# First phase of a two-block network on one core: column sums on VectorE, another order of modulation and h, the first two products row by row of h, the step sizes' chain in five steps

## The chip, the cores and the metric
The kernel runs on one core of one Trainium2 chip. The metric is the time of one execution on the device, in microseconds; smaller is better. Three runs of the kernel before gave 2241.81, 2244.04 and 2248.78 us.

## What is computed
Two blocks one after the other on 512 tokens of 1024 features, in float32. The first block's beginning is what the change touches:
```python
mod = silu(c) @ w_mod + b_mod              # six vectors of 1024 (shift, scale, gate, twice)
mod_c = silu(c_ctx) @ w_mod + b_mod        # the same for the context
h_lat = rmsnorm(x, norm1_g) * (1 + sc1) + sh1         # 512 tokens
h_ctx = rmsnorm(ctx, norm1_g) * (1 + csc1) + csh1     # 256 tokens
p = h @ w_in                               # z | xbc | dt | q | k | v | gates
xbc = silu(dwconv3(p[xbc]))                # 3072 channels, of them xs 2048, B 512, C 512, in four groups
dt = softplus(p[dt] + dt_bias)             # 64 step sizes a token
la = dt * -exp(a_log)                      # log decays, summed in chunks of 128 tokens
```
Then follow, for each of four groups, a bidirectional scan over chunks (ten states, four output chunks), window attention, the merge, a convolutional FFN, and a second block with three branches. All of that is the same in both kernels.

## The kernel before
Features lie on the partitions, tokens on the free axis; LT is 512 latent plus 256 context tokens. Each weight is split in two float32r parts, whi (a cast by ScalarE, line 1171) and wlo (a subtraction by GpSimd, line 2389), and so is h (hT_h by ScalarE, line 1190; hT_l by VectorE, line 1634, or GpSimd, line 2406, by turns). A product is three matmuls for each 128x128 of weights: whi·hi, whi·lo, wlo·hi (lines 760 to 762; 776 to 778 for the narrow dt). One xbc block is 8 rows of h x 2 column ranges (512 and 256) x 3, 48 matmuls. Weights come in blocks of 128x1024 (512 KB) into raww, a ring of RAWS = 4 slots; a slot is free when GpSimd has made wlo, or, for the modulation (not split, line 893), when TensorE has read it. whi and wlo have PAIRS = 3 slots. SyncE issues the loads (line 2562).

order() writes one list of steps, and every engine goes through this list in order and does its part of each step; semaphores carry the rest. So what stands behind a step in the list waits for it on each engine that has a part in it. merge() mixes two lists of steps by costs given in SHARE. plan.upto[t] says up to which block the split parts are to be made before step t, and SyncE loads RAWS blocks further, at steps that own a block.

The list of the first phase: init; norm1 (eight squares on ScalarE, line 1185, each with six column sums on TensorE, line 790, two instructions each); rms (VectorE reduces and takes the inverse root, lines 1640 to 1660, with a power on GpSimd, line 2398; TensorE spreads it over the partitions, line 799); then for each modulation j of 0 to 3 four blocks mod(j, n), modt (ScalarE copies the row, line 1228), xnorm (after j = 0; eight multiplications on VectorE, line 1845), modsel (TensorE turns the row, line 901) and modout (VectorE, lines 1851, 1857; for j = 2 and 3 it makes A1, the scale of h). 0 and 1 are shifts, 2 and 3 scales; 0 and 2 serve rows 0 to 3 of h, 1 and 3 rows 4 to 7. Then h1(0) to h1(7): hv = A1·x + shift on VectorE (lines 1869, 1870; rows 1, 4, 7 on ScalarE, lines 1236, 1237), its cast and its low part. Then four steps dt merged with the six xbc products of group 0:
```text
dt0  xbc0  xbc1  taps0 conv0  dt1  xbc2  taps1 conv1  xbc3  dt2
taps2 conv2  xbc4  taps3 conv3  dt3  xbc5  taps4 conv4  taps5 conv5
```
dt0 is the narrow product, dt1 (line 911) turns it and holds the whole softplus chain of VectorE and ScalarE (lines 1878 to 1886, 1694 to 1707), dt2 the cumulated sums (lines 916 to 918, 1890 to 1896), dt3 turns these (line 923), copies them (line 1899) and has ScalarE store them with eight DMAs (lines 1261, 1265). taps (lines 1199, 1686, 1689) and conv (1288, 1917) are the depthwise convolution and silu; taps reads the product's PSUM banks and frees them. The products take banks in turn out of four (0, 1, 2, 7), two for each xbc block (one for xbc5), so a product waits for the taps of the one two places before.
Behind it stand the transpositions xt, bt, the ten states of group 0 (line 947; VectorE lines 1734, 1937, 1942) with xbc(1,0) and xbc(1,1) among them, then the four chunks with cap (1958), decay (1313), cbm, cscale (1964), scale (1970), out (967 to 970), keep (1978) and xbc(1,2) to xbc(1,5) among them.

## Time and profile before
| | |
|---|---|
| runs | 2241.81, 2244.04 (median), 2248.78 us |
| profiled execution | 2248.61 us, its span 2247.3 us, mean granted clock 0.959 |
| busy | TensorE 2067.4, VectorE 1058.7, ScalarE 860.4, GpSimd 819.7 us |
| chain that ended last | TensorE 79%, VectorE 11%, ScalarE 4%, DMA 2% |
| DMA | 235.65 MB, mean 105 GB/s |

The span runs from the first to the last instruction of the program; the execution's own time is 1.3 us longer. A row of a timeline gives the start, the time from the first start to the last end of equal instructions in a row, the engine, the line, and in brackets how long the engine had been idle and what ended that. "PEclk" is the clock granted to TensorE, as a share of 2.4 GHz: 0.50 is 1.2 GHz. In a row of stages each engine has its busy time and its count of instructions.

### The profile page before, as it was taken

The page shows a single profiled execution, that of the slowest core. Times are in us where ns is not written, and L with a number is a line of the kernel's source. Part 1 is how long each engine was busy: PE and PEld are TensorE (multiplying, and loading weights), DVE is VectorE, ACT ScalarE, POOL GpSimd, SP SyncE. Part 2 cuts the span into 40 slices and gives each one's busy share as a digit, 9 for nine tenths or more (in the row PEclk, how much of TensorE's full clock was granted, in tenths as well). Part 3 has the DMA queues.
Part 4 walks back from the last instruction along what each step waited for, and adds up shares of the span by engine and source line. Part 5 has one row for each costly group of instructions (what it writes and reads, how often), then busy time and mean ns, then how long its engine had stood idle before and what let it go on. Part 6 is the DMA issues. An engine that isn't in the chain of part 4 may idle for free.

```text
span 2247.3 us, 28706 instructions
## 1 busy us (share of the span) xinstructions
PE 2067.4 (92%) x11668; PEld 1673.7 (74%) x11668; DVE 1058.7 (47%) x1735; ACT 860.4 (38%) x1561; POOL 819.7 (36%) x455
## 2 busy tenths in 40 slices
PE   6777999998999999999899999988889988989997
PEld 5565778786877787888787888876667766768886
DVE  1437776858555554542344442137544664521112
ACT  1333444444444444323343443233544443422221
POOL 0321121211353322456444444443531451554442
PEclk8788999999999999999999999989999999989998
DMA  6231544545321112523334333334121222333331
GB/s 218 82 124 52 185 160 159 162 152 184 127 71 38 38 48 83 180 94 103 94 114 143 101 100 94 96 120 127 47 68 53 83 60 84 97 97 96 94 101 63
DMA packets 89252, 235.65 MB, mean 105 GB/s; under 512 B 27424, under 2 KB 30624, under 8 KB 88224
## 3 DMA queue, kind: packets, MB, share of 16 engines
q1 hardware_dynamic: 85712, 225.16, 31.3%
q10 hardware_dynamic: 3408, 8.65, 1.0%
q8 instruction: 92, 1.51, 0.3%
q14 instruction: 40, 0.33, 0.0%
HBM read 220.51 MB, written 12.19 MB: 104 GB/s over the span
## 4 chain that ended last, share of the span: by engine, by line
PE 79%; DVE 11%; ACT 4%; DMA 2%; issue 1%; POOL 1%; ACTq 0%; SPq 0%; DVEq 0%; POOLq 0%
PE ps L760 20%; PE ps L761 20%; PE ps L762 20%; PE ps L1053 1%; PE ps L1112 1%; PE ps L947 1%; PE ps L1040 1%; PE ps L1028 1%; PE ps L893 1%; PE ps L790 1%; PE ps L969 1%; PE ps L967 1%; PE ps L968 1%; PE ps L1131 1%; PE ps L970 1%
## 5 line engine op out<-in xcount | busy, mean ns | idle before, releaser
L2389 POOL TENSOR_TENSOR wlo<-raww,whi 128x1024 fp32r<-128x1024 f32 (+2 forms) x254 | 593.8, 2344 | 1003.7 <-ACT whi L1171 999.3
L1171 ACT CAST whi<-raww 128x1024 fp32r<-128x1024 f32 (+2 forms) x284 | 285.0, 1006 | 262.9 <-PE ps L762 190.0
L760 PE MATMUL ps<-hT_h,whi 128*128 128x512 f32 (+1 forms) x704 | 268.7, 382 | 22.3 <-DVE xsc__81 L1689 19.0
L762 PE MATMUL ps<-hT_h,wlo 128*128 128x512 f32 (+1 forms) x704 | 259.6, 369 | 0.0
L761 PE MATMUL ps<-hT_l,whi 128*128 128x512 f32 (+1 forms) x704 | 259.5, 369 | 0.0
L760 PE MATMUL ps<-H_h,whi 128*128 128x512 f32 x480 | 192.3, 401 | 18.0 <-POOL wlo L2389 9.6
L761 PE MATMUL ps<-H_l,whi 128*128 128x512 f32 x480 | 188.6, 393 | 0.0
L762 PE MATMUL ps<-H_h,wlo 128*128 128x512 f32 x480 | 188.1, 392 | 0.0
L760 PEld LDWEIGHTS ps<-hT_h,whi 128*128 128x128 f32 x704 | 135.7, 193 | 49.7 <-DVE xsc__81 L1689 20.0
L761 PEld LDWEIGHTS ps<-hT_l,whi 128*128 128x128 f32 x704 | 135.4, 192 | 23.6 <-issue 2.9
L762 PEld LDWEIGHTS ps<-hT_h,wlo 128*128 128x128 f32 x704 | 135.0, 192 | 22.2
L1727 DVE SCALAR_TENSOR_TENSOR gt<-gt,ps 128x512 f32<-128x512 f32 x40 | 27.5, 687 | 254.3 <-PE ps L762 254.3
L760 PE MATMUL ps<-h_h,whi 128*128 128x512 f32 x336 | 132.1, 393 | 0.8 <-ACT mk L1450 0.8
L761 PE MATMUL ps<-h_l,whi 128*128 128x512 f32 x336 | 131.0, 390 | 0.0
L762 PE MATMUL ps<-h_h,wlo 128*128 128x512 f32 x336 | 130.8, 389 | 0.0
L760 PEld LDWEIGHTS ps<-H_h,whi 128*128 128x128 f32 x480 | 91.5, 191 | 42.1 <-issue 12.1
L762 PEld LDWEIGHTS ps<-H_h,wlo 128*128 128x128 f32 x480 | 91.1, 190 | 19.6
L761 PEld LDWEIGHTS ps<-H_l,whi 128*128 128x128 f32 x480 | 91.3, 190 | 18.7 <-issue 0.5
L1313 ACT ACTIVATE ec<-ec,la 128x128 f32<-128x128 f32 x256 | 76.9, 388 | 58.5 <-DVE ec L1958 58.5
L1686 DVE SCALAR_TENSOR_TENSOR ua<-ps,vc,ua 128x511 f32<-128x511 f32 x44 | 33.0, 750 | 110.1 <-ACT ua L1199 110.1
L1712 DVE TENSOR_REDUCE small<-ps 128x1 f32<-128x513 f32 (+1 forms) x64 | 48.3, 755 | 72.5 <-PE ps L1033 52.9
L760 PEld LDWEIGHTS ps<-h_h,whi 128*128 128x128 f32 x336 | 63.1, 188 | 15.8 <-issue 1.6
(500 smaller groups left out, 4678.7 us busy)
## 6 DMA issues: line engine op xcount, KB each, us to landing
ec<-csd SPq DMA_DIRECT2D x32, 1024.0 KB, 8.0
raww<-in_w_mod SPq DMA_DIRECT2D x48, 512.0 KB, 4.9
raww<-in_w_up SPq DMA_DIRECT2D x44, 512.0 KB, 3.7
raww<-in_w_xbc SPq DMA_DIRECT2D x24, 512.0 KB, 4.5
raww<-in_w_gl SPq DMA_DIRECT2D x24, 512.0 KB, 3.5
raww<-in_w_z SPq DMA_DIRECT2D x16, 512.0 KB, 4.4
raww<-in_w_g SPq DMA_DIRECT2D x16, 512.0 KB, 3.5
raww<-in_w_os SPq DMA_DIRECT2D x16, 512.0 KB, 3.6
```

Source lines behind the costliest of these rows:

```text
L760: e.matmul(o, whi[:, i, c], hi(k)[:, t0:t1], start=(k == 0), stop=False)
L761: e.matmul(o, whi[:, i, c], lo(k)[:, t0:t1], start=False, stop=False)
L762: last = e.matmul(o, wlo[:, i, c], hi(k)[:, t0:t1], start=False, stop=(k == kt - 1))
L790: last = e.matmul(ps[:, b, o:o + 1], x[:, t * 128:(t + 1) * 128], ones[:, 0:1], start=True, stop=True)
L893: last = e.matmul(ps[32 * q:32 * q + 32, b, 0:128], cs_[:, 4 * n + 2 * kk:4 * n + 2 * kk + 32], raww[:, p % RAWS, kk * 512 + q * 128:kk * ...
L947: e.matmul(ps[:, b, :], Btok[:, CHUNKS[d][n], :], xw[:, i, :], start=True, stop=True).then_inc(*ssd_done.mark(("state", g, d, n), ("free", ...
L1171: e.copy(whi[:, i, 0:n], raww[:, p % RAWS, 0:n]).then_inc(*w_high.mark(("high", p)))
L1313: last = e.activation(E[:, r, :], E[:, r, :], ACT.Exp, bias=la[:, c, h:h + 1])
L1686: e.scalar_tensor_tensor(out=dst[:, 1:T], in0=psum[:, 0:T - 1], scalar=V(names[0], m), in1=dst[:, 1:T], op0=ALU.mult, op1=ALU.add).then_in ...
L1712: e.tensor_reduce(sm[:, 1:2], S, AXX, ALU.max, negate=True).then_inc(*v_step.mark(event))
L1727: e.scalar_tensor_tensor(out=x, in0=x, scalar=1.0, in1=psum, op0=ALU.add, op1=ALU.mult).then_inc(*v_moved.mark(*events))
L2389: e.tensor_tensor(wlo[:, i, 0:n], raww[:, p % RAWS, 0:n], whi[:, i, 0:n].bitcast(F32), ALU.subtract).then_inc(*p_wlow.mark(("split", p), ( ...
```

## The change
1. Squares: the seven additions of the eight squares go to VectorE (acc1), and TensorE forms six column sums of the total in a step total of its own. The reduction on VectorE goes.
2. Order: modulation 0, then 2, 1, 3, with norm, root, xnorm (now one step a row), h rows and their split in between. The modulations 0 to 3 take banks 3 and 4.
3. bring: the blocks of w_dt and of xbc(0,0) are loaded before the last four modulation blocks and split there. Before dtx 2 no other block is split.
4. dtx 0 to 3 replace the narrow product and xbc(0,0): each takes two rows of h for both. w_dt's low part is written beside its high part into whi, so one matmul with hi gives whi·hi in rows 0 to 63 and wlo·hi in rows 64 to 127, and dt1 adds the halves as it turns them (12 matmuls for 6 transposes).
5. The chain of the step sizes is cut: 0 copies, 1 turn, abs, exp, 2 one plus, ln, 3 reciprocal up to ln step, 4 the cumulated sums, 5 their turn and store.
6. SHARE has other costs for groups 0 and 1, and one xbc step of group 1 instead of two among the states.

The list becomes (numbers as in the code; m is mod):
```text
init norm1 m(0,0) m(0,1) m(0,2) total m(0,3) modt0 m(2,0) m(2,1) modsel0 modout0 rms m(2,2) m(2,3) modt2
xnorm0 xnorm1 m(1,0) modsel2 modout2 m(1,1) h0 xnorm2 m(1,2) h1 xnorm3 m(1,3) modt1 h2 xnorm4 bring h3 xnorm5
m(3,0) modsel1 modout1 m(3,1) xnorm6 dtx0 m(3,2) xnorm7 m(3,3) modt3 dtx1 modsel3 modout3 h4 h5 dtx2 h6 h7 dtx3
dt0 xbc1 taps0 conv0 dt1 xbc2 taps1 conv1 dt2 xbc3 taps2 conv2 dt3 xbc4 taps3 conv3 dt4 xbc5 dt5 taps4 conv4 taps5 conv5
xt4 xt5 xbc(1,0) bt xt0..3, ten states, cb cap decay cap decay xbc(1,1) cbm cscale scale out(0,0) taps(1,0) conv(1,0)
xbc(1,2) ... keep0 out(0,1) ... xbc(1,3) ... out(0,2) xbc(1,4) ... xbc(1,5) keep2 out(0,3) ... xt(1,4) and on as before
```
```diff
+         "state": 9.6, "cap": 0.54, "cbm": 0.9, "scale": 3.8, "out": 4.8, "keep": 1.45, "xbc": 4.0, "taps": 0.05,
+         "conv": 2.5, "z": 1.65, "zgate": 0.77, "zsum": 0.7, "mod": 2.25, "score": 1.66, "pt": 1.12, "pv": 0.82,
...
 def ssd_states(g):
-    t = [(SHARE["xt"], [("xt", g, 4), ("xt", g, 5)]), (SHARE["bt"], [("bt", g)]), (SHARE["xt"], [("xt", g, c) for c in range(4)])]
...
 def xbc_steps(g):
...
-    o = [("init",), ("norm1",), ("rms", "in")]
-    for j in range(4):
-        o += [("mod", j, n) for n in range(4)] + [("modt", j)] + ([("modsel", j - 1), ("modout", j - 1)] if j else [("xnorm",)])
-    o += [("modsel", 3), ("modout", 3)]
-    o += [("h1", k) for k in range(8)]
-    o += merge([(8.0, [("dt", i)]) for i in range(4)], xbc_steps(0))
+    mod = lambda j: [[("mod", j, n)] for n in range(4)]
+    a, b, c, d = mod(0), mod(2), mod(1), mod(3)
+    o = [("init",), ("norm1",)] + a[0] + a[1] + a[2] + [("total", "in")] + a[3] + [("modt", 0)]
+    o += b[0] + b[1] + [("modsel", 0), ("modout", 0), ("rms", "in")] + b[2] + b[3] + [("modt", 2), ("xnorm", 0), ("xnorm", 1)]
+    o += c[0] + [("modsel", 2), ("modout", 2)] + c[1] + [("h1", 0), ("xnorm", 2)] + c[2] + [("h1", 1), ("xnorm", 3)]
+    o += c[3] + [("modt", 1), ("h1", 2), ("xnorm", 4), ("bring",), ("h1", 3), ("xnorm", 5)]
+    o += d[0] + [("modsel", 1), ("modout", 1)] + d[1] + [("xnorm", 6), ("dtx", 0)] + d[2] + [("xnorm", 7)] + d[3] + [("modt", 3), ("dtx", 1)]
+    o += [("modsel", 3), ("modout", 3), ("h1", 4), ("h1", 5), ("dtx", 2), ("h1", 6), ("h1", 7), ("dtx", 3)]
+    o += merge([(SHARE["dt"], [("dt", i)]) for i in range(6)], xbc_steps(0))
     x = xbc_steps(1)
-    o += [("load", 0), ("load", 1)] + merge(ssd_states(0), x[:2]) + merge(ssd_chunks(0), x[2:])
...
-    if s == ("dt", 0):
-        return [(("w_dt", 0, 0, 512), 512, True)]
+    if s == ("bring",):
+        return [(("w_dt", 0, 0, 512), 512, True), (("w_xbc", 0, 0, 1024), 1024, True)]
...
+        for t, s in enumerate(self.order):
             mine = blocks_of(s)
             if mine:
...
+                if t < start:
+                    n = base if s[0] == "bring" else n
+                else:
+                    n = max(n, min(self.split_at[more - 1] + 1 if more <= len(self.split_at) else len(self.blocks), base + RAWS - 1))
+                load = max(load, n + RAWS, base + RAWS)
             elif s[0] == "duo" and s[3] == 7:
                 n = max(n, min(self.split_at[done + AHEAD - 1] + 1, base + RAWS - 1))
...
+                n = self.split_at[done + AHEAD - 2] + 1
+                load = n + RAWS
             self.upto.append(n)
+            self.loads.append(load)
         spans = {s: t for t, s in enumerate(self.order)}
         a, b = spans["s5tab", 0], spans["fence", "glu"]
...
+        sq1, acc1 = sbuf("sq1", [P, 4, LT], 136), sbuf("acc1", [P, LT], 148)
...
-                elif k == "norm1":
-                    for j in range(8):
-                        add_up("in", j, ["in"])
+                elif k == "total" and s[1] == "in":
+                    b = bank(("stat", s[1]), (5,))
+                    PE.wait_ge(at("squares", s[1]))
+                    for t in range(6):
+                        last = e.matmul(ps[:, b, t:t + 1], acc1[:, t * 128:(t + 1) * 128], ones[:, 0:1], start=True, stop=True)
...
+                elif k == "dtx":
+                    x = ("xbc", 0, 0)
+                    pd, px = plan.first["dt", 0], plan.first[x]
+                    if s[1] == 0:
+                        banks = [bank((u, t0), ring_of_gemms[0]) for u in (("dt", 0), x) for t0, _ in ALL]
+                        PE.wait_ge(at("split", pd))
+                        PE.wait_ge(at("split", px))
+                    else:
+                        banks = [bank_of((u, t0)) for u in (("dt", 0), x) for t0, _ in ALL]
+                    wd, wx = plan.pair[pd] % PAIRS, plan.pair[px] % PAIRS
+                    hi, lo = PAIR["hT"]
+                    two = (2 * s[1], 2 * s[1] + 1)
+                    end = s[1] == 3
+                    for q in two:
+                        PE.wait_ge(at("pair", "hT", q))
+                        c = slice(q * 128, (q + 1) * 128)
+                        for (t0, t1), b in zip(ALL, banks[2:]):
+                            o = ps[:, b, 0:t1 - t0]
+                            e.matmul(o, whi[:, wx, c], hi(q)[:, t0:t1], start=(q == 0), stop=False)
+                            e.matmul(o, whi[:, wx, c], lo(q)[:, t0:t1], start=False, stop=False)
+                            last = e.matmul(o, wlo[:, wx, c], hi(q)[:, t0:t1], start=False, stop=(q == 7))
+                            if q == 7:
+                                last.then_inc(*gemm_done.mark(("gemm", x, t0), *[("used", px)] * (t1 == LT)))
+                    for (t0, t1), b in zip(ALL, banks[:2]):
+                        for q in two:
+                            if q:
+                                e.matmul(ps[0:64, b, 0:t1 - t0], whi[:, wd, q * 128:q * 128 + 64], lo(q)[:, t0:t1], start=False, stop=False)
+                            last = e.matmul(ps[:, b, 0:t1 - t0], whi[:, wd, q * 128:q * 128 + 128], hi(q)[:, t0:t1], start=(q == 0), stop=(q == 7))
+                            if q == 0:
+                                e.matmul(ps[0:64, b, 0:t1 - t0], whi[:, wd, 0:64], lo(0)[:, t0:t1], start=False, stop=False)
+                        if end:
+                            last.then_inc(*gemm_done.mark(("gemm", ("dt", 0), t0), *[("used", pd)] * (t1 == LT)))
+                elif k == "xbc" and s[1:] == (0, 0):
+                    pass
                 elif k == "dt":
-                    if s[1] == 0:
-                        narrow(s, 64, "hT", ALL)
-                    elif s[1] == 1:
+                    if s[1] == 1:
                         b = bank("dtok", (4,))
                         PE.wait_ge(at("dt rows"))
                         for c in range(6):
-                            last = e.transpose(ps[:, b, c * 64:c * 64 + 64], dtT[:, c * 128:c * 128 + 128], ident[0:64, 0:64])
+                            e.matmul(ps[:, b, c * 64:c * 64 + 64], dtT[:, c * 128:c * 128 + 128], ident[:, 0:64], start=True, stop=False)
+                            last = e.matmul(ps[:, b, c * 64:c * 64 + 64], dtT[:, c * 128:c * 128 + 128], ident[:, 64:128], start=False, stop=True)
                         last.then_inc(*turned.mark(("dt turned",)))
...
+                    o = halves(i)[:, :, 0:64] if p == plan.first["dt", 0] else whi[:, i, 0:n]
+                    x = raww[:, p % RAWS, 0:n]
+                    e.copy(o, x.rearrange("p (k c) -> p k c", c=64) if p == plan.first["dt", 0] else x).then_inc(*w_high.mark(("high", p)))
...
+                        ACTE.wait_ge(at("modulation turned", {2: 0, 1: 2, 3: 1}.get(j, j - 1)))
...
-                            e.copy(dtT[:, t0:t1], ps[0:64, bank_of((s, t0)), 0:t1 - t0]).then_inc(
+                            e.copy(dtT[:, t0:t1], ps[:, bank_of((s, t0)), 0:t1 - t0]).then_inc(
...
+                        ACTE.wait_ge(at("abs", "dt"))
+                        e.activation(flat(csm), flat(csm), ACT.Exp, scale=-1.0).then_inc(*a_func.mark(("exp abs", "dt")))
+                    elif s[1] == 2:
+                        ACTE.wait_ge(at("one plus", "dt"))
+                        e.activation(flat(etot), flat(wdec), ACT.Ln).then_inc(*a_func.mark(("ln", "dt")))
+                    elif s[1] == 3:
                         ACTE.wait_ge(at("step kept off zero"))
                         e.activation(lndt[:, :, :], lndt[:, :, :], ACT.Ln).then_inc(*a_func.mark(("ln step",)))
-                    elif s[1] == 2:
...
+                elif k == "norm1":
+                    for j in range(1, 8):
+                        DVE.wait_ge(at("square", "in", j - 1) + at("square", "in", j))
+                        after_last()
+                        e.tensor_tensor(acc1[:, :], acc1[:, :] if j > 1 else sq1[:, slot("sq1", ("in", 0)), :],
+                                        sq1[:, slot("sq1", ("in", j)), :], ALU.add).then_inc(
+                            *v_made.mark(("free", "sq1", ("in", j)), *[("free", "sq1", ("in", 0))] * (j == 1), *[("squares", "in")] * (j == 7)))
                 elif k == "xnorm":
+                    j = s[1]
...
-                    for j in range(8):
-                        e.tensor_tensor(xin[:, j, :], xin[:, j, :], r, ALU.mult).then_inc(
-                            *v_moved.mark(("x normed", j), *[("out of", ("rms", "in"))] * (j == 7)))
+                    e.tensor_tensor(xin[:, j, :], xin[:, j, :], r, ALU.mult).then_inc(
+                        *v_moved.mark(("x normed", j), *[("out of", ("rms", "in"))] * (j == 7)))
...
-                        softplus("dt", flat(dt_), flat(csm), flat(wdec), flat(etot))
+                        after_last()
+                        e.scalar_tensor_tensor(out=u, in0=x, scalar=-1.0, in1=x, op0=ALU.mult, op1=ALU.max).then_inc(*v_step.mark(("abs", "dt")))
+                    elif s[1] == 2:
+                        DVE.wait_ge(at("exp abs", "dt"))
+                        e.tensor_scalar(w, u, 1.0, None, ALU.add).then_inc(*v_step.mark(("one plus", "dt")))
+                        after_last()
+                        e.scalar_tensor_tensor(out=u, in0=w, scalar=-1.0, in1=u, op0=ALU.add, op1=ALU.subtract).then_inc(*v_step.mark())
+                    elif s[1] == 3:
+                        DVE.wait_ge(at("ln", "dt"))
+                        after_last()
+                        e.reciprocal(w, w).then_inc(*v_step.mark())
+                        after_last()
+                        e.scalar_tensor_tensor(out=u, in0=u, scalar=-1.0, in1=w, op0=ALU.mult, op1=ALU.mult).then_inc(*v_step.mark())
...
-                    e.tensor_tensor(wlo[:, i, 0:n], raww[:, p % RAWS, 0:n], whi[:, i, 0:n].bitcast(F32), ALU.subtract).then_inc(
-                        *p_wlow.mark(("split", p), ("raw free", p)))
+                    o, x, h = wlo[:, i, 0:n], raww[:, p % RAWS, 0:n], whi[:, i, 0:n]
+                    if p == plan.first["dt", 0]:
+                        o, x, h = halves(i)[:, :, 64:128], x.rearrange("p (k c) -> p k c", c=64), halves(i)[:, :, 0:64]
...
-                if plan.upto[t] and s in plan.first:
-                    load_weights(plan.upto[t] + RAWS)
+                if s in plan.first or s == ("dtx", 2):
+                    load_weights(plan.loads[t])
```

## Rows read from the trace of the kernel before
**Rows 1.** The page: engines' busy; the splits' groups (busy, mean ns of one).
```profile
PE 2067.4 (92%) x11668; PEld 1673.7 (74%) x11668; DVE 1058.7 (47%) x1735; ACT 860.4 (38%) x1561; POOL 819.7 (36%) x455
...
L2389 POOL TENSOR_TENSOR wlo<-raww,whi 128x1024 fp32r<-128x1024 f32 (+2 forms) x254 | 593.8, 2344 | 1003.7 <-ACT whi L1171 999.3
...
L1171 ACT CAST whi<-raww 128x1024 fp32r<-128x1024 f32 (+2 forms) x284 | 285.0, 1006 | 262.9 <-PE ps L762 190.0
```
**Rows 2.** Stages: length, PE, PEld, DVE, ACT, POOL busy, PEclk, DMA share, GB/s.
```profile
18.20:35.40 17.20, 14.54 (x67) 14.26 (x67) 0.88 (x5) 0.84 (x1) 1.33 (x1) 1.00 0.00 1
...
40.40:63.10 22.70, 14.71 (x200) 8.90 (x192) 4.87 (x9) 2.36 (x5) 3.50 (x2) 0.50 0.93 328
...
63.10:81.30 18.20, 10.48 (x23) 4.31 (x24) 9.76 (x15) 11.07 (x15) 7.90 (x6) 0.50 0.13 45
...
77.90:81.30 3.40, 3.32 (x8) 1.48 (x9) 0.79 (x1) 1.86 (x3) 2.38 (x2) 0.50 0.00 0
...
84.50:92.84 8.34, 8.34 (x50) 7.38 (x49) 0.00 (x0) 1.32 (x2) 2.39 (x1) 1.00 0.35 117
...
92.80:166.60 73.80, 59.32 (x313) 50.12 (x311) 30.27 (x52) 27.19 (x45) 14.26 (x6) 0.91 0.28 93
...
166.60:191.40 24.80, 18.88 (x68) 10.93 (x69) 17.00 (x25) 1.38 (x2) 2.34 (x1) 0.98 0.16 54
...
191.40:254.80 63.40, 53.82 (x434) 47.53 (x432) 57.24 (x78) 34.65 (x89) 10.61 (x4) 0.90 0.40 125
...
322.00:2247.00 1925.00, 1810.92 (x10009) 1470.37 (x10008) 887.74 (x1467) 746.71 (x1337) 760.52 (x424) 0.97 0.31 100
```
**Rows 3.** Timeline, 9 to 63 us: column sums, spread, xnorm, A of modout 3.
```profile
9.27 20.64 PE L790 MATMUL ps<-cst,sq 128*128 128x1 f32 x96 [9.27 <-DMA cst<-in_consts]
...
32.58 2.93 PE L799 MATMUL ps<-cst,nst 128*128 128x128 f32 x12 [2.66 <-DVE nst L1646]
...
35.55 7.00 DVE L1845 TENSOR_TENSOR xin<-xin,ps 128x768 f32<-128x768 f32 x8 [3.02 <-PE ps L799]
...
61.83 1.39 DVE L1857 SCALAR_TENSOR_TENSOR A<-modS,vc 128x8 f32<-128x8 f32 x1
```
**Rows 4.** Timeline of the h rows: low parts, the last narrow matmul's wait.
```profile
64.90 0.96 DVE L1634 TENSOR_TENSOR hT_l<-hv,hT_h 128x768 fp32r<-128x768 f32 x1 [0.90 <-ACT hT_h L1190]
...
67.02 1.81 POOL L2406 TENSOR_TENSOR hT_l<-hv,hT_h 128x768 fp32r<-128x768 f32 x1 [3.82 <-ACT hT_h L1190]
...
67.71 1.93 DVE L1634 TENSOR_TENSOR hT_l<-hv,hT_h 128x768 fp32r<-128x768 f32 x1 [1.07 <-ACT hT_h L1190]
...
80.80 0.68 PE L776 MATMUL ps<-hT_h,whi 128*64 128x512 f32 x1
```
**Rows 5.** Timeline of PE: products of group 0 behind waits, dt3's transposes.
```profile
115.24 0.56 PE L760 MATMUL ps<-hT_h,whi 128*128 128x512 f32 x1 [4.84 <-DVE xsc__81 L1689]
...
132.18 0.77 PE L760 MATMUL ps<-hT_h,whi 128*128 128x512 f32 x1 [5.45 <-DVE xsc__81 L1689]
...
142.36 0.60 PE L923 MATMUL ps<-cst,csm 128*64 128x128 f32 x4
...
152.62 0.50 PE L760 MATMUL ps<-hT_h,whi 128*128 128x512 f32 x1 [3.30 <-DVE BTs L1689]
```
**Rows 6.** Timeline of ACT: a table load, the issues of dt3's eight stores.
```profile
103.62 1.28 ACT L1196 ACT_TABLE_LOAD   x1
...
143.72 2.66 ACTq L1261 DMA_DIRECT2D csd<-csT  x4
...
147.08 2.10 ACTq L1265 DMA_DIRECT2D csd<-ecsT  x4
```
**Rows 7.** Timeline of DVE in the states: the wait behind xbc(1,1).
```profile
184.64 0.69 DVE L1942 TENSOR_TENSOR st<-stt__90,ps 128x512 f32<-128x512 f32 x1 [5.91 <-PE ps L947]
```
**Rows 8.** Chunks: a stage as in rows 2, and PE's wait for taps(1,0).
```profile
199.50:250.20 50.70, 47.37 (x360) 41.57 (x360) 49.36 (x67) 27.45 (x69) 10.61 (x4) 0.92 0.47 147
...
202.03 0.77 PE L760 MATMUL ps<-hT_h,whi 128*128 128x512 f32 x1 [8.69 <-DVE xsc__81 L1689]
```

69 lines of the change are left out of this document (41 added, 28 removed), and 4 rows, old and new, of the table SHARE.

## The prediction
> **What bounds the kernel now.** I read the engines' totals first: TensorE is busy for 92% of the span, no other engine for half of it [rows 1]. The table of stages comes second. After 322 us TensorE works 1811 us of 1925, at 0.97 of its clock, and nothing of the change lies there; those 1925 us are carried over as they are. What an edit of the first phase can reach lies before about 255 us, and there the table shows different stages [rows 2]. (a) 18.2 to 35.4 us: the DMA share is 0.00. All four slots of raww hold modulation blocks that TensorE has not read, since it forms column sums until 29.9 and then waits for the root. (b) 40.4 to 63.1: DMA at 0.93, TensorE at half clock: the modulation is paced by its weights. (c) 63.1 to 81.3: the eight rows of h are made, TensorE busy 10.5 of 18.2. (d) 92.8 to 166.6: five products of group 0 and the step sizes' chain, TensorE busy 59 of 74. (e) 166.6 to 191.4: ten states, a chain on VectorE. (f) 191.4 to 254.8: four chunks, VectorE busy 57 of 63. The waits in the timelines come third; they give the single terms.
>
> **Part 1: from the start to the end of the first xbc product, 92.8 us now.** Removed: the 48 column sums (96 instructions) that fill 9.3 to 29.9 [rows 3]. Added: seven additions of 128x768 on VectorE. A subtraction of that shape with both operands in SBUF takes 0.96 [rows 4], so 6.7 us; some of them fit before the second half of x has landed, and I let the last end at 18.2, when the four modulation blocks are there too, for DMA goes quiet at 18.2 [rows 2]. Six sums remain, 12 instructions at 20.64/96 = 0.215, so 2.6 us: 20.8.
> Modulation 0 and half of 2 are multiplied as they land. The root stands behind modout 0 on VectorE, at about 23.5, and costs 2.5 (29.9 to 32.6 now, less the reduction that goes); the spread takes 2.9 at full clock, up to 5.9 at half [rows 3]; I take 4.2: 30.2. On TensorE mod(2,2) and mod(2,3) are queued behind this spread, and with them the slots, so DMA pauses again for some 3 us.
> Then VectorE works in order: two rows of xnorm (7.00/8 = 0.88 each), modout 2 with its A (1.4) [rows 3], at about 33.8. Rows of h take 17.7/8 = 2.2 each now (63.1 to 80.8 [rows 4]), and an xnorm mostly fits into VectorE's waits for ScalarE's casts: rows 0 to 2 by 40.4. On ScalarE the casts of w_dt and of the first xbc block stand behind row 2, on GpSimd their low parts follow, for 1024 columns 1.0 and 2.34, for 512 about half of each [rows 1]: 1.5 and 2.3 after row 2, dtx 0 may start at 44.3.
> One dtx covers two rows. For xbc it is six 128x512 and six 128x256 matmuls; for dt the wlo product now sits in the idle 64 columns of a pass, so it is four of each instead of six. At half clock eight 128x512 take 3.4 us, 0.43 each [rows 2], a 256 half of it: 10 x 0.64 = 6.4 us for one dtx, and 3.2 at full clock. The clock was back at 81.3, after 3.3 us of work [rows 2]. So a dtx behind idle time costs about 4.9, one behind work 3.2. dtx 0 ends at 49.2. The last two modulation blocks reuse the slots of w_dt and xbc, freed at 42 to 44, and land at 47 to 49: 50.5. modsel 3 is queued behind dtx 1: 53.9. modout 3 and its A: 55.7. Rows 4 to 7: four times 2.2, and 1.0 for the cast of block 18 and 1.1 for its low part, which are queued before row 6's cast and row 7's low part: 10.9. dtx 2 runs from 62.4 to 67.3, dtx 3 to 70.5. I take **71**, against 92.8: **21.8 gained**. Bounds: 14 more blocks (7.1 MB) after 18.2 at stage (b)'s 328 GB/s [rows 2] end at 40, and with the tail (1 + 2 + 10.9 + 3.2) the product ends at 57; with all four dtx at half clock it ends at 80.
>
> **Part 2: from there to the first state product, 73.8 us now.** The step sizes' chain stood in one step between xbc products, and the taps that free TensorE's banks were queued behind it. TensorE waits 4.84, 5.45 and 3.30, and after each wait the product takes 10.2 (132.18 to 142.36 [rows 5]) where an undisturbed one takes 8.34 [rows 2]: 13.6 + 5.6 = 19.2 us. With five steps the longest piece is the one from the reciprocal to the clamp, some 5.5 us, and the taps come in time within 8.34. Exp, Tanh and Ln alternate more often, two more table loads of 1.28 on ScalarE [rows 6], which is busy 27 of 74 us [rows 2]: hidden; 2.6 without this cover.
> Two waits are new or larger. (1) xbc(0,1) takes the banks of dt, which ScalarE copies only after dtx 3: 1.1 us (hidden by xbc(0,0) now). (2) The last step (transposes, csT, eight stores that ScalarE issues) now stands behind xbc(0,5) instead of before it. ScalarE needs 5.5 us for it (143.72 to 149.18 [rows 6]), and taps(0,4), whose bank xbc(1,0) takes, are queued behind. From the transposes' end (142.96) to xbc(1,0) at 152.62 are 9.7 us [rows 5], and 6.4 of them are TensorE's work now: xbc(0,5) and a transposition. After the change only the transposition, 1.0, lies in it: a wait of 8.7, and a cold product behind (+1.9). Twelve instead of six narrow products turn dt: +0.5. Sum: -19.2 + 1.1 + 8.7 + 1.9 + 0.5 = **7.0 gained**. Bounds: 18 gained if wait (2) doesn't come, 2 lost if old waits stay.
>
> **Part 3: the ten states, 24.8 us now.** xbc(1,1) moves out of them. VectorE waits 5.91 for a state queued behind this product on TensorE [rows 7]; else it needs 2.0 a state. **5.9 gained.** TensorE then idles between all states, but the stage shows 0.98 of the clock with it [rows 2]; I cost that at nothing. Bounds 2 and 7.5.
>
> **Part 4: the four chunks, 63.4 us now.** xbc(1,1) comes here, between the caps and the first output, into the 8.69 that TensorE waits there for taps(1,0) behind ScalarE's decays [rows 8]. TensorE's work: 53.8 busy now [rows 2], less 1.9 for the product that was cold behind that wait, plus 8.4, is 60.3. VectorE's is 57.2, and between 199.5 and 250.2 it is busy 49.4 of 50.7 [rows 8]. Two full engines, each in order: I add 1.2, 61.5, **1.9 gained**. Bounds: 60.3 and 68.
> The steps behind are the same, and nothing there goes by absolute time.
> The Trainium skill has a rule that speaks against more work on VectorE ("SBUF — State Buffer", section "SBUF: two separate sides"): a VectorE operation with two SBUF inputs and a GpSimd operation that reads SBUF exclude each other for the whole instruction. The trace agrees: the same low part takes 0.96 alone and 1.93 when GpSimd has begun one before it [rows 4]. For the seven additions it changes nothing, since GpSimd is idle then; by it each new meeting in parts 1 and 4 would cost about 1 us, which the bounds hold.
>
> **Sum.** 21.8 + 7.0 + 5.9 + 1.9 = 36.6 us. The profiled execution has a span of 2247.3 us and took 2248.6; it would be 2210.7 and 2212.0. It lies 4.6 above the median of the runs, so against 2244.0 the forecast is **2207.5 us**.
>
> **The rivals.** *A, the weights' stream decides the first phase.* The slots never run out and part 1 ends near 60, or wait (2) isn't there: 11 us more in either case, **2196.5**. For it: the stream could end at 40. Against: root and spread stand before mod(2,2) on TensorE, and two slots wait for GpSimd. *B, a cold first phase.* The clock stayed at 0.50 from 63.1 to 81.3 with TensorE busy 10.5 of 18.2 us [rows 2]. If products row by row keep it there, every dtx costs 6.4, +9.4, and a few us of VectorE's meetings with GpSimd come in part 4: **2221**. The Trainium skill ("TensorE: Matmul & The Clock Gate", section "Part 1: The HAM clock gate") says that half rate is the default and that activity lifts it; by it, the removal of the column sums leaves TensorE at half clock from the start, where stage (a) shows full clock, and B is what follows. *C, the modulation isn't ahead.* The slots stay taken, by the spread in the queue and by the wait for GpSimd's low parts, mod(3,3) still ends near 57, and wait (2) eats the rest: 5 us gained, **2239**. *D, slower.* One mechanism: the clock does not come back behind dtx 3, and products of 8.4 us in parts 2 and 4 run at half. Each costs 8.4 more; from the fifth on (42 against 36.6) the kernel is slower than before, seven give **2266**. Against it: from 84.5 dense products held 1.00, and (d) to (f) 0.90 and more [rows 2].
>
> **How the numbers follow.** Forecast 0.47 (2200 to 2216), A 0.23 (below 2200), B 0.20, C 0.06, D 0.04. The range takes in B and most of A with their bounds, **2190 to 2227**, and leaves out C, D and the lowest part of A. A measurement of this kernel can tell about 0.3% (7 us) from no change: faster 0.92, same 0.05, slower 0.03.
>
> **What would show it.** Part 1: w_mod's first 16 issues end near 44, the A of modout 3 ends near 55.7, the first xbc product near 71. Part 2: no wait of TensorE over 2 us between xbc(0,1) and xbc(0,5), then one of 8 to 9 before xbc(1,0), behind ScalarE's eight stores. Part 3: ten states in 19 us, without a wait of 5.9. Part 4: no wait of 8.7, 60 to 63 us. The prediction is wrong if the work behind xt(1,4) takes another time than now, or if a dense stretch shows a granted clock of 0.50.

## The result and the profile after

The changed kernel took 2208.76 us (median of four runs, 2205.08 to 2210.52), the kernel before, measured beside it, 2244.35; the ratio is 0.9837, 95% interval 0.9817 to 0.9857. The forecast was 2207.5, range 2190 to 2227.

The profiled execution of after is the fastest of its runs, 2205.1 us with a span of 2203.7, while that of before (2248.6) was 4.3 above its median. So the two traces differ by 43.5 us, the medians by 35.6. The page of after, busy times and the group of GpSimd's splits (compare [rows 1]: no engine's work has changed by more than 2% of itself):
```profile
PE 2035.2 (92%) x11586; PEld 1651.1 (75%) x11586; DVE 1060.8 (48%) x1741; ACT 862.6 (39%) x1563; POOL 821.7 (37%) x455
...
L2483 POOL TENSOR_TENSOR wlo<-raww,whi 128x1024 fp32r<-128x1024 f32 (+2 forms) x253 | 594.3, 2355 | 945.3 <-ACT whi L1237 941.0
```
The stages of after (columns as in [rows 2]): the first two reach to the root's spread, the next two to the copies of dt, then one each for the prediction's parts 2, 3 and 4, and the rest.
```profile
0.00:15.50 15.50, 0.00 (x0) 0.00 (x1) 5.35 (x20) 6.15 (x9) 0.30 (x5) 1.00 0.93 327
15.50:30.50 15.00, 12.06 (x126) 9.86 (x130) 3.93 (x9) 1.70 (x3) 1.33 (x1) 1.00 0.79 276
30.50:58.40 27.90, 16.85 (x207) 13.05 (x206) 15.29 (x21) 6.80 (x11) 7.63 (x4) 0.76 0.63 217
58.40:73.40 15.00, 9.99 (x40) 7.92 (x40) 3.52 (x6) 7.59 (x12) 6.66 (x3) 0.77 0.12 37
73.40:140.10 66.70, 58.13 (x329) 50.23 (x329) 30.84 (x52) 30.61 (x48) 16.76 (x7) 0.95 0.34 111
140.10:156.90 16.80, 11.95 (x21) 3.48 (x22) 14.86 (x24) 0.41 (x1) 0.00 (x0) 0.90 0.13 44
156.90:218.40 61.50, 58.50 (x482) 52.12 (x480) 59.82 (x79) 35.72 (x90) 13.80 (x5) 1.00 0.42 138
...
218.40:2203.70 1985.30, 1867.73 (x10391) 1514.48 (x10390) 927.15 (x1533) 773.61 (x1392) 775.22 (x430) 0.97 0.32 102
```
The DMA share tells the main thing: where before had 17 us at 0.00 [rows 2], after has 0.93, 0.79 and 0.63 up to 58.4. The four parts against their forecasts, in us:

| part | before | after | forecast |
|---|---|---|---|
| 1, to the first product's end | 92.8 | 73.4 | 71 |
| 2, to the first state product | 73.8 | 66.7 | 66.8 |
| 3, ten states | 24.8 | 16.8 | 18.9 |
| 4, four chunks, to xt(1,4) | 63.4 | 61.5 | 61.5 |
| sum | 254.8 | 218.4 | 218.2 |
| behind it | 1992.5 | 1985.3 | 1992.5 |

Part 1 in the timeline of after (PE, DVE, POOL, ACT; columns as in [rows 3]):
```profile
15.53 2.27 PE L921 MATMUL ps<-raww,cs__56 128*32 128x128 f32 x32 [15.53 <-DMA raww<-in_w_mod]
...
19.01 2.72 PE L855 MATMUL ps<-cst,acc 128*128 128x1 f32 x12
...
27.58 2.93 PE L824 MATMUL ps<-cst,nst 128*128 128x128 f32 x12 [2.61 <-DVE nst L1716]
30.44 1.76 PE L921 MATMUL ps<-raww,cs__56 128*32 128x128 f32 x48
...
42.48 2.43 DVE L1943 TENSOR_SCALAR hv<-xin,A,modS 128x256 f32<-128x256 f32 x1
...
42.24 2.52 POOL L2483 TENSOR_TENSOR wlo<-raww,whi 128x1024 fp32r<-128x1024 f32 x1
...
47.64 0.79 PE L952 MATMUL ps<-hT_h,whi 128*128 128x512 f32 x1 [4.18 <-DVE xin L1918]
...
58.20 0.17 DVE L1930 SCALAR_TENSOR_TENSOR A<-modS,vc 128x8 f32<-128x8 f32 x1
...
72.50 0.86 ACT L1310 COPY dtT<-ps 128x512 f32<-128x512 f32 x2 [5.46 <-PE ps L961]
```
The modulation starts at 15.5 instead of 35.4 and the spread is through at 30.5. The first dtx then waits 4.18 us, and not for its weights: these are split at 42.24 + 2.52 = 44.76. It waits for VectorE's last xnorm (L1918), which reads bank 7. Part 2 has the wait that was forecast, before xbc(1,0), behind ScalarE's eight issues and the activations of taps(0,4) (PE, then ACT and its queue):
```profile
117.73 1.09 PE L994 MATMUL ps<-cst,xsc__82 128*128 128x128 f32 x8 [0.78 <-DVE csT L1990]
125.67 0.80 PE L785 MATMUL ps<-hT_h,whi 128*128 128x512 f32 x1 [6.85 <-DVE BTs L1755]
...
117.71 2.71 ACTq L1332 DMA_DIRECT2D csd<-csT  x4
...
121.12 2.10 ACTq L1336 DMA_DIRECT2D csd<-ecsT  x4
123.27 1.23 ACT L1265 ACTIVATE BTs<-ps,vc 128x512 f32<-128x512 f32 x2 [2.18 <-issue]
```
The waits of [rows 5] (4.84, 5.45, 3.30), of [rows 7] (5.91) and of [rows 8] (8.69) are gone.

### The profile page after: what moved, and what is told of

It is laid out like the page before. It is cut to its first block, busy times and chain, and to the rows that moved or that the text cites. A ratio compares the mean times of both kernels' runs of the same rounds, so it can differ in the third digit from the quotient of the medians.

```text
span 2203.7 us, 28555 instructions
## 1 busy us (share of the span) xinstructions
PE 2035.2 (92%) x11586; PEld 1651.1 (75%) x11586; DVE 1060.8 (48%) x1741; ACT 862.6 (39%) x1563; POOL 821.7 (37%) x455
## 4 chain that ended last, share of the span: by engine, by line
PE 79%; DVE 12%; ACT 4%; DMA 1%; issue 1%; POOL 1%; ACTq 0%; SPq 0%; DVEq 0%; POOLq 0%
PE ps L785 20%; PE ps L786 20%; PE ps L787 20%; PE ps L1117 1%; PE ps L1104 1%; PE ps L1176 1%; PE ps L1011 1%; PE ps L1092 1%; PE ps L921 1%; PE ps L1033 1%; DVE ec L2049 1%; PE ps L1031 1%; PE ps L1195 1%; PE ps L1032 1%; PE ps L1158 1%
## 5 line engine op out<-in xcount | busy, mean ns | idle before, releaser
L785 PE MATMUL ps<-hT_h,whi 128*128 128x512 f32 (+1 forms) x688 | 261.1, 379 | 7.4 <-DVE BTs L1755 6.8
L787 PE MATMUL ps<-hT_h,wlo 128*128 128x512 f32 (+1 forms) x688 | 252.4, 367 | 0.0
L786 PE MATMUL ps<-hT_l,whi 128*128 128x512 f32 (+1 forms) x688 | 252.3, 367 | 0.0
L1778 DVE TENSOR_REDUCE small<-ps 128x1 f32<-128x513 f32 (+1 forms) x64 | 48.3, 755 | 72.5 <-PE ps L1097 52.9
```

Of the source, the lines that this page charges most:

```text
L785: e.matmul(o, whi[:, i, c], hi(k)[:, t0:t1], start=(k == 0), stop=False)
L786: e.matmul(o, whi[:, i, c], lo(k)[:, t0:t1], start=False, stop=False)
L787: last = e.matmul(o, wlo[:, i, c], hi(k)[:, t0:t1], start=False, stop=(k == kt - 1))
L1778: e.tensor_reduce(sm[:, 1:2], S, AXX, ALU.max, negate=True).then_inc(*v_step.mark(event))
```

## Experiments

Each kernel below was profiled, so they can be compared by four places in their timelines as well as by the whole time: the start of dt's copies (ScalarE, L1310 in after), the first state product, the first product cb behind the states, and xt(1,4), behind which the step list is the same everywhere. The whole time is uncertain by some 4 us, the places by up to 1.9: after, e1, e7 and e8 have the same list up to dt's copies, which start at 72.5, 74.4, 74.0 and 74.2. What differs first between these four is when TensorE gets its full clock: at 31.0 us in after, at 32.8 to 33.3 in the other three. There the three modulation blocks behind the spread take 2.76 to 2.79 instead of the 1.76 above (TensorE's timeline of e1):
```profile
30.11 2.79 PE L923 MATMUL ps<-raww,cs__56 128*32 128x128 f32 x48
```
and GpSimd's low part of the first xbc block ends 0.7 to 0.9 later than in after. The clock also rose late in e3 and e11, and early in e2 and e10.

| run | median us | ratio to before (95%) | dt copies | state | cb | xt(1,4) | behind |
|---|---|---|---|---|---|---|---|
| before | 2244.35 | 1 | 82.0 | 166.6 | 191.4 | 254.8 | 1992.5 |
| after | 2208.76 | 0.9837 (0.9817–0.9857) | 72.5 | 140.1 | 156.9 | 218.4 | 1985.3 |
| e1_store_late | 2202.65 | 0.9799 (0.9779–0.9818) | 74.4 | 136.2 | 152.9 | 214.5 | 1988.2 |
| e2_turn_first | 2203.20 | 0.9803 (0.9777–0.9829) | 68.8 | 136.2 | 153.0 | 214.5 | 1988.8 |
| e3_bank7_free | 2206.98 | 0.9820 (0.9795–0.9845) | 70.9 | 138.5 | 156.0 | 216.8 | 1988.9 |
| e4_root_behind_mod2 | 2206.01 | 0.9816 (0.9791–0.9841) | 73.2 | 141.0 | 158.5 | 219.2 | 1985.9 |
| e5_sums_on_pe | 2224.06 | 0.9903 (0.9881–0.9925) | 87.8 | 155.5 | 173.0 | 233.8 | 1989.1 |
| e6_before_sums_dve | 2238.72 | 0.9960 (0.9946–0.9973) | 75.0 | 159.7 | 184.5 | 248.1 | 1989.2 |
| e7_chain_one_step | 2218.33 | 0.9876 (0.9849–0.9903) | 74.0 | 151.9 | 169.5 | 230.2 | 1985.8 |
| e8_old_states | 2217.97 | 0.9874 (0.9847–0.9901) | 74.2 | 142.0 | 166.4 | 229.5 | 1986.7 |
| e9_products_behind_h | 2203.27 | 0.9806 (0.9788–0.9824) | 66.7 | 134.1 | 150.9 | 212.4 | 1988.5 |
| e10_three_edits | 2196.36 | 0.9778 (0.9765–0.9791) | 65.8 | 127.5 | 144.3 | 205.8 | 1987.4 |
| e11_four_edits | 2196.52 | 0.9778 (0.9765–0.9791) | 67.3 | 129.1 | 146.6 | 207.4 | 1987.8 |
| e12_before_again | 2246.46 | – | 83.2 | 167.8 | 192.7 | 256.2 | 1988.9 |

In before and e6 the copies of dt come before the first xbc product (half of them, for the second follows at 84.7 in before), so this column compares only kernels with dtx.

**e1_store_late**: the wait in part 2.
```diff
+    o.remove(("dt", 5))
+    o.insert(o.index(("conv", 0, 4)) + 1, ("dt", 5))
```


> The changed kernel with one step moved: dt5 (turn and store of the sums) stands behind conv(0,4) in the list, so ScalarE makes taps(0,4) before it issues the eight stores. Theory (the wait of 6.85 us before xbc(1,0) is the store's issues in front of the taps): this wait falls under 1 us, the cold product behind it is gone (+1.9), the first state product starts at 131 to 133 us instead of 140.1, and 8 us reach xt(1,4) (210). Rival (the states need the stored sums anyway): the wait only moves to the first state, which starts at 138 to 140; xt(1,4) within 2 us of 218.4.


From the copies of dt to the first state product it takes 61.8 us instead of 67.6: 5.8 gained, where about 8 were expected (3.9 at xt(1,4), since this execution's copies of dt started 1.9 later). No wait before xbc(1,0) is left; what remains, and was not expected, in TensorE's timeline of e1, is the wait of the transposes for the copy of the turned sums:
```profile
121.36 1.36 PE L996 MATMUL ps<-cst,xsc__82 128*128 128x128 f32 x8 [2.54 <-DVE csT L1992]
```
The position of this one step in the list was the cause of the 6.85.

**e2_turn_first**: dtx 1 stood before modsel 3.
```diff
-    ... d[3] + [("modt", 3), ("dtx", 1)]
-    o += [("modsel", 3), ("modout", 3), ("h1", 4), ("h1", 5), ("dtx", 2), ...
+    ... d[3] + [("modt", 3)]
+    o += [("modsel", 3), ("modout", 3), ("dtx", 1), ("h1", 4), ("h1", 5), ("dtx", 2), ...
```


> The changed kernel with dtx 1 behind modsel 3 and modout 3 instead of before them. Theory (A of rows 4 to 7 is late because its turn is queued behind dtx 1 on TensorE): A ends near 55 instead of 58.4 and everything behind is 3.4 us earlier, xt(1,4) at 215. Rival (TensorE has no gap to put dtx 1 in): 0 to 1 us.


A of modout 3 comes 3.6 us earlier than the 58.20 of after, the copies of dt 3.7, xt(1,4) 3.9 (VectorE's timeline of e2):
```profile
54.61 0.17 DVE L1930 SCALAR_TENSOR_TENSOR A<-modS,vc 128x8 f32<-128x8 f32 x1
```
Two matmuls of 8 columns decide when rows 4 to 7 of h begin; a product of 3.6 us in front of them passes on in full.

**e3_bank7_free**: what the first dtx waits for.
```diff
-                        spread(("rms", n), 3, LT, (6,), at("root", n))
+                        spread(("rms", n), 3, LT, (5,), at("root", n))
```
The spread then lies in banks 5 and 6 instead of 6 and 7.


> The changed kernel with the spread of the root in banks 5 and 6 instead of 6 and 7. Theory (dtx 0 starts at 47.6 and not at 44.8, where its low part is ready, because its fourth bank, 7, is part of the spread that xnorm(7) reads last): dtx 0 starts at 44.8 and xt(1,4) comes 2 to 2.9 us earlier. Rival (the last two modulation blocks then set the pace, their slots are freed by GpSimd): dtx 0 earlier, the A of modout 3 unchanged at 58.4, xt(1,4) unchanged.


TensorE's timeline of e3, the first matmul of dtx 0:
```profile
45.55 0.77 PE L952 MATMUL ps<-hT_h,whi 128*128 128x512 f32 x1 [1.82 <-POOL wlo L2483]
```
dtx 0 now waits for GpSimd's low part, and no longer for the bank. The copies of dt come only 1.6 us earlier than in after, less than the 2 to 2.9 expected and inside the scatter of the places. But the clock rose late here, so the low part ended 0.7 later (45.45). Beside e1, e7 and e8, where the clock rose as late, dtx 0 starts 2.8 to 3.0 us earlier and the copies come 3.1 to 3.5 earlier. So the bank was the cause, and about 3 us is what it was worth. The whole times of e3 and after can't be told apart.

**e4_root_behind_mod2**: do the slots behind the spread cost anything?
```diff
-    o += b[0] + b[1] + [("modsel", 0), ("modout", 0), ("rms", "in")] + b[2] + b[3] + ...
+    o += b[0] + b[1] + [("modsel", 0), ("modout", 0)] + b[2] + b[3] + [("rms", "in")] + ...
```


> The changed kernel with the root and its spread behind mod(2,3) instead of before mod(2,2). Theory (the spread in TensorE's queue holds two raw slots and stops the DMA): the blocks of w_dt and xbc are issued 3 us earlier, the A of modout 3 ends 2 to 3 us earlier, xt(1,4) near 216. Rival (the path through part 1 is VectorE's xnorm and h rows, which wait for the spread): everything 1.5 to 2 us later, xt(1,4) near 220.


mod(3,3) ends at 54.54 (54.13 in after) and xt(1,4) is 0.8 later, which is inside the scatter: no gain, and no loss that could be told either. The spread comes no later than in after (27.74 against 27.58), and GpSimd's low part ends at 44.60 (44.76 in after), since ScalarE casts these weights behind row 2 of h in both. So the slots held by the spread cost nothing that shows. The run also tells something of the clock, since here TensorE's granted clock rose early. Two stages of e4:
```profile
18.50:21.80 3.30, 2.50 (x48) 2.22 (x44) 0.00 (x0) 0.27 (x1) 0.00 (x0) 1.00 0.91 339
21.80:32.00 10.20, 7.89 (x80) 5.90 (x80) 2.12 (x7) 0.27 (x1) 1.33 (x1) 0.50 0.85 280
```
and TensorE's timeline in them:
```profile
18.50 1.50 PE L855 MATMUL ps<-cst,acc 128*128 128x1 f32 x12
...
27.74 2.93 PE L824 MATMUL ps<-cst,nst 128*128 128x128 f32 x12
```
The spread takes 2.93 in a stretch that is recorded at 0.50, exactly as in after (27.58) and in before [rows 3], and the six sums take 1.50 in a stretch at 1.00 where they take 2.72 in after. I come back to this below.

**e5_sums_on_pe**: the changed kernel with the 48 column sums on TensorE.
```diff
-    o = [("init",), ("norm1",)] + a[0] + a[1] + a[2] + [("total", "in")] + a[3] + [("modt", 0)]
+    o = [("init",), ("norm1",)] + a[0] + a[1] + a[2] + a[3] + [("modt", 0)]
...
+                elif k == "norm1":
+                    for j in range(8):
+                        add_up("in", j, ["in"])
```
(and in VectorE's program the seven additions go, the reduction comes back)


> The changed kernel with the 48 column sums back on TensorE (no additions on VectorE, the reduction back), all else as changed. Theory (the sums hold TensorE until 29.9 us and with it the raw slots and the root): the first modulation product starts at 30 instead of 15.5, the root 5 us later, the last modulation block and the A of modout 3 about 8 us later, first state product near 148, and about 8 us are lost at xt(1,4). Rival (the later weights' stream or VectorE catches up): less than 3 us at xt(1,4).


The column sums and the spread in TensorE's timeline of e5:
```profile
9.13 20.64 PE L815 MATMUL ps<-cst,sq 128*128 128x1 f32 x96 [9.13 <-DMA cst<-in_consts]
...
41.75 2.93 PE L824 MATMUL ps<-cst,nst 128*128 128x128 f32 x12 [2.93 <-DVE nst L1713]
```
15.4 us later at xt(1,4), twice what I expected. I had priced the sums as in the old order, where the root stands before the modulation. In the new one it stands behind six of its blocks, so with the sums at 29.7 all of it starts 14.2 later (29.70 against 15.53) and the spread 14.2 later (41.75 against 27.58).

**e6_before_sums_dve**: the same edit alone, in the kernel before.
```diff
-                    for j in range(8):
-                        add_up("in", j, ["in"])
+                    for t in range(6):
+                        last = e.matmul(ps[:, b, t:t + 1], acc1[:, t * 128:(t + 1) * 128], ones[:, 0:1], start=True, stop=True)
```
(and the seven additions on VectorE)


> The kernel before with this one part of the change: squares added on VectorE, six column sums on TensorE. Theory: all of the first phase starts 8.2 us earlier (29.9 to 21.7), first state product at 158.4 instead of 166.6, xt(1,4) at 246.6 instead of 254.8. Rival (without the sums TensorE is at half clock and the modulation slower): under 4 us.


The six sums, the spread and the first modulation in TensorE's timeline of e6:
```profile
19.02 2.69 PE L830 MATMUL ps<-cst,acc 128*128 128x1 f32 x12 [19.02 <-DVE acc L1843]
24.05 2.93 PE L799 MATMUL ps<-cst,nst 128*128 128x128 f32 x12 [2.33 <-DVE nst L1649]
26.91 3.48 PE L896 MATMUL ps<-raww,cs__56 128*32 128x128 f32 x64
```
Alone it gains 6.7 us at xt(1,4) (8.2 expected; 2238.7, ratio 0.996), less than half of the 15.4 that it is worth in the new order. Additions on VectorE and modulation ahead of the root are worth more together.

**e7_chain_one_step**: the step sizes' chain in one step and where it stood.
```diff
+    for i in (2, 3, 4, 5):
+        o.remove(("dt", i))
+    i = o.index(("dt", 1)) + 1
+    o[i:i] = [("dt", 2), ("dt", 3)]
+    o.insert(o.index(("xbc", 0, 3)) + 1, ("dt", 4))
+    o.insert(o.index(("xbc", 0, 5)), ("dt", 5))
```


> The changed kernel with the step sizes' chain in one piece behind dt1 and the sums' steps where the kernel before has them. Theory (the forecast's part 2): waits of 4.8, 5.4 and 3.3 us come back, that of 6.85 goes, 7 us are lost, first state product at 147. Rival (the new wait eats what the cut gains): within 2 us of 140.1.


Waits of products in TensorE's timeline of e7:
```profile
99.56 0.77 PE L791 MATMUL ps<-hT_h,whi 128*128 128x512 f32 x1 [5.02 <-DVE xsc__82 L1761]
...
117.19 0.77 PE L791 MATMUL ps<-hT_h,whi 128*128 128x512 f32 x1 [5.45 <-DVE xsc__82 L1761]
137.90 0.50 PE L791 MATMUL ps<-hT_h,whi 128*128 128x512 f32 x1 [3.31 <-DVE BTs L1761]
```
The three waits of [rows 5] are back to within 0.2 us, the one of 6.85 is gone, and from the copies to the first state product it takes 77.9 instead of 67.6: 10.3 lost, against 7 expected (the first state product comes at 151.9, not 147).

**e8_old_states**: two products of group 1 before and among the states again.
```diff
-SHARE = {"dt": 2.4, "x1": 1.2, "state0": 10.56, "xbc0": 5.76, "xbc1": 13.1, "taps0": 0.05, "taps1": 0.01,
-         "conv0": 4.0, "conv1": 2.4, "xt0": 2.6, "bt0": 0.91, "cap0": 0.54, "out0": 11.93, "xt": 2.6, "bt": 0.55,
+SHARE = {"dt": 2.4, "x1": 2, "xbc0": 5.76, "taps0": 0.05,
+         "conv0": 4.0, "xt": 2.6, "bt": 0.55,
```


> The changed kernel with the old list from the states of group 0 on (xbc(1,1) among the states). Theory: the states take 24.8 us instead of 16.8 and the chunks 63.4 instead of 61.6, so xt(1,4) at 228. Rival (the chunks, with VectorE at 95%, take back what the states gain): xt(1,4) at 221 or less.


The states and the chunks of e8 as stages:
```profile
142.00:166.40 24.40, 18.48 (x69) 10.79 (x70) 16.66 (x24) 1.37 (x2) 2.34 (x1) 1.00 0.15 53
166.40:229.50 63.10, 53.05 (x434) 46.87 (x432) 55.07 (x79) 34.45 (x89) 12.22 (x4) 0.89 0.37 126
```
and its timeline in the states (DVE, POOL):
```profile
143.83 2.51 DVE L1800 TENSOR_TENSOR xw<-xtok,wdec 128x512 f32<-128x512 f32 x1
...
143.45 2.34 POOL L2483 TENSOR_TENSOR wlo<-raww,whi 128x1024 fp32r<-128x1024 f32 x1 [7.36 <-ACT whi L1237]
```
7.6 us lost in the states, 1.6 in the chunks, and 1.9 before them, which is the copies of dt starting 1.7 later. Beside the wait of 5.9 for the product (5.89 here) the states hold a second one that I had not read: the multiplication xw, 0.69 elsewhere, takes 2.51 when GpSimd's split of the next block has begun 0.38 before it, and TensorE waits for it. The trace of before has the same collision, in VectorE's timeline:
```profile
168.44 2.51 DVE L1734 TENSOR_TENSOR xw<-xtok,wdec 128x512 f32<-128x512 f32 x1
```
In after no split falls into the states. The 1.8 us between 2.51 and 0.69 are most of the 2.1 by which part 3 came out shorter than forecast.

**e9_products_behind_h**: are products row by row needed?
```diff
+    for i in range(4):
+        o.remove(("dtx", i))
+    i = o.index(("h1", 7)) + 1
+    o[i:i] = [("dtx", 0), ("dtx", 1), ("dtx", 2), ("dtx", 3)]
```


> The changed kernel with all four steps dtx behind h1(7) in the list; nothing is left out. After it, dtx 2 and 3 ended at 72.5 us, and dtx 0 and 1 were done before 61. Theory (what lies in the tail behind the last row of h counts in full): the low part of row 7 still comes near 70, TensorE was idle for most of 54 to 70 and is at half clock when the four products begin; the first costs about 4.9, the others 3.2, so dt's copies come near 70 + 14.5 = 84.5 less what rows 0 to 6 allow before the last low part (three products may run as their rows come, yet in the list they stand behind all h steps only on VectorE and ScalarE, not on TensorE, whose queue holds nothing between modsel 3 and dtx 0): if TensorE takes dtx 0 as soon as modsel 3 is through, near 55, the copies come within 3 us of 73, since dtx 0 to 2 fit between 55 and 69. Modsel 3 in turn is no longer behind dtx 1: the A of modout 3 comes some 4 us earlier, near 54.5, and the copies 2 to 4 us EARLIER than 73. I hold this second reading: -2 to -4 us at the end of xt(1,4) (total about 2205). Rival (products row by row among the modulations are what gained in this part): without them the copies come 8 us later, near 81, and the kernel takes about 2217.


The stage of the four products in e9:
```profile
50.80:66.70 15.90, 15.90 (x80) 13.33 (x80) 4.79 (x8) 6.75 (x9) 6.05 (x3) 0.85 0.29 110
```
and A of modout 3 in VectorE's timeline:
```profile
51.28 0.17 DVE L1934 SCALAR_TENSOR_TENSOR A<-modS,vc 128x8 f32<-128x8 f32 x1
```
6 us earlier than after at xt(1,4), against the rival that gave +8, and more than the 2 to 4 that I held. Behind h in the list the products delay neither mod(3,2), mod(3,3) nor modsel 3 on TensorE. The two blocks now wait for nothing but their weights, until 46.4 and 49.0, and A comes 6.9 us earlier than in after. TensorE, which has no part in h, begins with dtx 0 at 50.9 anyhow and is busy for the whole 15.9 us, while rows 4 to 7 are made beside it. And the cast and low part of block 18, which the list ties to dtx 2, no longer stand between the rows: from A to the last low part it takes 9.9 us, not 11.8.

**e10_three_edits**: e1, e2 and e3 together.
```diff
+    o.remove(("dt", 5))
+    o.insert(o.index(("conv", 0, 4)) + 1, ("dt", 5))
-    ... d[3] + [("modt", 3), ("dtx", 1)]
+    ... d[3] + [("modt", 3)]
+    o += [("modsel", 3), ("modout", 3), ("dtx", 1), ("h1", 4), ...
-                        spread(("rms", n), 3, LT, (6,), at("root", n))
+                        spread(("rms", n), 3, LT, (5,), at("root", n))
```


> The changed kernel with three edits together: the step sizes' last step behind conv(0,4), dtx 1 behind modout 3, and the root's spread in banks 5 and 6. Alone they gave, at the end of xt(1,4), 3.9 us (218.4 to 214.5, of it 5.8 from the copies of dt on), 3.9 and 1.6 us. Theory (three separate waits, additive): dt's copies near 73.2 - 3.7 - 1.6 = 68, from there to the first state product 61.8 instead of 67.6; the end of xt(1,4) 10 to 11 us before the changed kernel's, near 207.5, and the kernel at about 2198 (ratio to before 0.979). Rival 1 (the chain of the rows of h is what is left once modout 3 comes early; the bank's edit then gives nothing more): near 209, 2200. Rival 2 (the weights' stream gives the time back: the blocks of group 1 come no earlier, so the products from xbc(0,2) on wait for them): the end of xt(1,4) stays at 213 to 214.5, 2203.


2196.36 us over five runs: it beats both kernels, 2.2% below before, and its interval lies wholly below that of after. 12.6 us at xt(1,4): 6.7 up to the copies of dt (the turn 3.7 alone; the bank 1.6 against after, about 3 against kernels whose clock rose as late as e3's), 5.9 from there on (5.8 alone). So the three waits are separate and, within the scatter, add up. The stage of dtx 2 and 3, for what follows:
```profile
58.60:66.70 8.10, 6.48 (x34) 5.10 (x34) 0.83 (x1) 2.75 (x6) 4.87 (x3) 1.00 0.22 67
```

**e11_four_edits**: e10, and dtx 1 to 3 behind h.
```diff
+    for i in range(1, 4):
+        o.remove(("dtx", i))
+    i = o.index(("h1", 7)) + 1
+    o[i:i] = [("dtx", 1), ("dtx", 2), ("dtx", 3)]
```


> The kernel of the three edits with dtx 1, 2 and 3 behind h1(7) in the list; dtx 0 stays where it is; nothing is left out. Block 18's cast (1.04) and low part are made before dtx 2 in the list, so they move behind row 7 as well. Theory (in the run with all products behind h the last low part ended 9.9 us after the A of modout 3 instead of 11.8, because this cast and low part no longer stand between the rows): from A 51.8 the last low part now ends at 61.7 instead of 63.5, dtx 3 takes 3.2 behind it, so dt's copies start near 65 instead of 65.8; the low part of block 18 is ready by 65 (2.4 to 3.1 behind row 7's), just in time for xbc(0,1). Gain at the end of xt(1,4) 0.8 to 1.8 us, from 205.8 to 204 to 205; total about 2195, which the time alone can't tell from 2196.4. Rival (this low part is now late for xbc(0,1)): TensorE waits 1 to 2 us at xbc(0,1) and the end of xt(1,4) is 206 or later.


The stage of dtx 2 in e11:
```profile
60.10:63.60 3.50, 3.50 (x10) 2.79 (x11) 0.76 (x1) 1.82 (x3) 2.52 (x2) 0.55 0.02 5
```
and its first matmul in TensorE's timeline:
```profile
60.09 0.80 PE L958 MATMUL ps<-hT_h,whi 128*128 128x512 f32 x1 [2.22 <-POOL hT_l L2505]
```
The rows do take 9.9 us instead of 11.8, as expected, but from A to the copies of dt it is 14.2 in both kernels. The clock rose later here than in e10 (at 32.5 against 30.6; the three modulation blocks took 2.69 against 1.75) and the first low part ended 1.0 later, which accounts for most of the 1.6 at xt(1,4). The 1.9 won in the rows was lost again on TensorE, which found its clock at half when dtx 2 began at 60.1 (0.55 in that stretch; in e10 1.00, in the row above). No gain, and neither of the two expectations: xbc(0,1) doesn't wait for its low part.

**e12_before_again**: does what lies behind xt(1,4) differ between the kernels?


> The kernel before, unchanged, profiled a second time, for what lies behind xt(1,4): the step list is the same in both kernels there, yet the profiled execution of before spent 1992.5 us on it and the ten kernels built on the changed one 1985.4 to 1989.1. Theory (the length of this part differs from execution to execution by how long each fall of TensorE's clock lasts; it does not belong to the kernel): this execution takes 1986 to 1990 us there, with 99 to 106 us at half clock instead of 116.1, and its whole time is nearer the median of 2244 than 2248.6 was; up to xt(1,4) it takes 254.8 within 1.5 us. Rival (before's order has a lasting effect on what lies behind): 1992 us or more again, and about 116 us at half clock.


The stage behind xt(1,4) in this second execution:
```profile
256.20:2245.10 1988.90, 1871.99 (x10391) 1516.16 (x10390) 931.59 (x1533) 773.73 (x1392) 773.89 (x430) 0.97 0.32 102
```
1988.9 us in a second execution of the same program, 3.6 less than in the first and within the 1985.3 to 1989.2 of the kernels with a new first phase. The length isn't a property of the kernel to within these 4 us. My cause for it did not hold: summed up from the clock records, TensorE was at half clock for 116.1 us behind xt(1,4) in both executions of before, against 99 to 113 in after, e9, e10 and e11. What else differs between two executions isn't settled. A lasting difference of some 3 us isn't excluded: the two executions of before average 1990.7, the eleven kernels built on the changed one 1987.5.

## Why the prediction was right

**Part 1** (forecast 21.8 gained, measured 19.4). Right: the order of events up to the spread, the additions hidden, the split of the first weights (44.3 against 44.8). The spread's end (30.2 against 30.5) was hit by luck: it began at 27.6 instead of 26.0 and took 2.93 instead of 4.2, since the 2.9 that I had read as its price at full clock is the price at half clock (see rival B). Wrong: "dtx 0 may start at 44.3". It started at 47.6. I followed its weights and its rows of h, but not its PSUM banks: the fourth bank of the products' ring, 7, is half of the root's spread, and VectorE reads that until the last xnorm. e3 shows this. All later steps keep the offset: the last modulation ends at 54.1 instead of 50.5, since it is queued behind dtx 0; A comes at 58.2 instead of 55.7; the product ends at 73.4 instead of 71. Two smaller terms nearly cancelled: A takes 0.17 us instead of the 1.39 of [rows 3], and the rows with block 18 take 11.8 instead of 10.9.

**The 1.39 for A** was not its price (0.17 in after). It was a collision: in before GpSimd's split runs from 60.86 to 63.20, and A from 61.83 to 63.22. e6 still has it (DVE, POOL):
```profile
54.80 1.38 DVE L1863 SCALAR_TENSOR_TENSOR A<-modS,vc 128x8 f32<-128x8 f32 x1
...
53.82 2.34 POOL L2395 TENSOR_TENSOR wlo<-raww,whi 128x1024 fp32r<-128x1024 f32 x1 [0.41 <-ACT whi L1174]
```
Both end at 56.2: VectorE's small operation waited for GpSimd's.

**Part 2** (forecast 7.0, measured 7.1). The three old waits went and the new one came, 6.85 instead of 8.7 (before, ScalarE still had a cast of 1.04 between the stores and the taps, which I carried over; in after this cast comes first); the wait for dt's copies was 0.53 instead of 1.1. e7 and e1 show both halves: the cut is worth 10.3 here, and the last step's place costs 5.8 of what it could be worth. The bound of 18 without the new wait was too high: e1, which removes it, gains 5.8 more, about 13 in all. The two more table loads were hidden.

**Part 3** (forecast 5.9, measured 8.0). The mechanism was right, the term too small: the collision of xw with GpSimd stood in the trace of before, and I had not read it.

**Part 4** (forecast 1.9, measured 1.9). The sum was right, by terms that offset each other: TensorE needed 58.5 and not 60.3, and VectorE, at 59.8 of 61.5, was nearer to being the bound than I said; it has 2.6 more than the 57.2 of before [rows 2]. Of these, 2.1 lie in the 24 multiplications of 128x1024 (37.0 against 34.9), beside which GpSimd now makes five low parts instead of four: one more meeting, which the prediction had put at about 1 us, in its bounds only.

**Sum.** 36.6 forecast, 36.4 measured at xt(1,4), 35.6 by the medians. That it fits within 1 us is luck: part 1 gave 2.4 less and part 3 2.1 more than forecast, and the places scatter by up to 1.9. The forecast said that it is wrong if the work behind xt(1,4) takes another time. In the profiled pair it does, by 7.2 us. A second execution of before makes 3.6 of them its own (e12); for the rest, what scatters from execution to execution and what lasts isn't separated. The medians, 35.6 apart, leave little room for the 7.2 on top of the 36.4.

**The rivals.** *A*, the stream of weights: no. TensorE waits for w_mod several times up to 41, but from 44.8 to 47.6 it is the bank that decides, and the last two blocks had landed when dtx 0 was through. The rival's other form, no wait (2), was priced at 11 us; e1 puts it at 5.8. *B*, a cold first phase: its reason was better than I made it, and it did not cost what I said. I had put against it that stage (a) shows full clock. It doesn't: the stages show 1.00 from the start of each trace up to the first change in its clock record. Of the 96 instructions of column sums each took 0.215 us [rows 3], as the six sums in after did (2.72/12 = 0.227), while in e4 they took 1.50/12 = 0.125 where 1.00 is recorded; and the spread takes 2.93 in before, in after and in e4's recorded 0.50. So TensorE was at half clock in stage (a), dense column sums and all, and in after until about the spread's end: a modulation block takes 1.1 at 15.5 (2.27 for two) and 0.59 at 30.4 (1.76 for three). The rule of the Trainium skill ("TensorE: Matmul & The Clock Gate", section "Part 1: The HAM clock gate"), that half rate is the default, agrees with these durations. It changed nothing in the gain, as the column sums had been at half clock before too. And with products row by row the clock did come back: dtx 0 and 2, behind idle time, ran mostly at 0.63 for a 512, dtx 1 and 3 at 0.40. dtx 0 took 5.4 us, dtx 1 3.6 and dtx 3 3.5, against the 4.9, 3.2 and 3.2 of the forecast. But to put the first of them among the modulations did not pay: e9, with all four behind h in the list, is 6 us earlier. *C*, modulation not ahead: no. e4 shows that the slots behind the spread cost nothing. *D*, half clock in dense stretches: no, parts 2 and 4 show 0.95 and 1.00.

## What to carry to other kernels

Where engines take their parts of one list in order, ask of each moved step what stands behind it on every engine, down to instructions of 0.3 us: a turn of two matmuls behind a product, or eight DMA issues in front of an activation, cost 4 to 6 us here, and moving these two steps and one bank gave 12.6. Follow a new consumer's destination as far as its inputs: the bank that it writes may be the last thing to come free. Before taking a duration from a trace as a price, look at what GpSimd did in that moment and at the clock of that stretch, by known durations rather than by the column alone.

## What the hardware showed that I had not expected

A VectorE operation with only one SBUF tensor input can wait for GpSimd too. The TENSOR_SCALAR that makes hv (float32, 128x256) took 2.43 from 42.48 on (row in the first section), until just behind the end of GpSimd's split at 44.76. Alone it takes, in VectorE's timeline of after:
```profile
32.99 0.55 DVE L1942 TENSOR_SCALAR hv<-xin,A,modS 128x512 f32<-128x512 f32 x1
33.45 0.41 DVE L1943 TENSOR_SCALAR hv<-xin,A,modS 128x256 f32<-128x256 f32 x1
```
So 256 more columns cost it 0.14 us, about half of the 0.27 that they cost an operation on two tensors (xw of 512 takes 0.69, a low part of 768 0.96 [rows 4]). The prediction cited the Trainium skill only for operations with two SBUF inputs; the Trainium skill ("SBUF — State Buffer", section "SBUF: two separate sides") names VectorE's two-port modes as well. The trace agrees as far as the wait and the halved price of a column go; that hv ran in such a mode is inferred from them. Three kinds of operation were caught in this way: this one, A (0.17 to 1.38) and xw (0.69 to 2.51).

The clock column shows 1.00 before the first recorded change, whatever the clock is. The same list can reach dt's copies 1.9 us apart, with the moment at which the clock rises as the first difference (31.0 against 32.8 to 33.3). And the same program can differ by 3.6 us over 1990 us of the same instructions.
